# Two convolutions of the next feed-forward step placed between VectorE's additions of the down product

## The chip, the cores and the metric

The kernel runs on one core of a Trainium2 chip. The metric is the device time of one execution in microseconds (us); three executions of the kernel before took 1811.97, 1813.63 and 1813.83 us. A core has TensorE (PE, matmuls into eight PSUM banks), VectorE (DVE), ScalarE (ACT), GpSimd (POOL) and SyncE (SP, which here only issues DMAs). Each engine works through its own list in order; between engines there are semaphores.

## The reference

One inference step of one layer over 1088 tokens (1024 of a new stream, 64 of a running one). After attention and a Conformer convolution comes the feed-forward part, which the change touches:

```python
x = x + (jax.nn.sigmoid(g_attn) * a + jax.nn.sigmoid(g_conv) * c) @ w_out
up, new_ffn = causal_dwconv(rmsnorm(x, norm2_g) @ w_up, ffn_buf, ffn_dw_w, ffn_dw_b)
gate, val = jnp.split(up, 2, axis=-1)
x = x + (jax.nn.silu(gate) * val) @ w_down
```

`w_up` is 1024 x 5632, `w_down` 2816 x 1024; the depthwise convolution has width 3, so its result at a token is a weighted sum of that token and the two before, plus a bias. A final RMSNorm gives the outputs.

## The kernel before

Channels lie on the 128 partitions and tokens along the free dimension. All matmul operands are split into a high and a low part, and each product is three matmuls: high x high and the two mixed ones.

The feed-forward part runs NF = 11 steps. Step i takes two gate tiles and two value tiles of 128 channels each, counted by tau: tau 0 and 2 are gate tiles, tau 1 and 3 value tiles. The tokens are cut into three pieces c of 364, 364 and 360. One *up job* (i, tau, c) is 24 matmuls (`up_product`, L1519) into bank (3 tau + c) mod 4. So there are 12 up jobs per step, and each waits until the bank it writes, used four jobs earlier, has been copied out. The *down product* of the step follows: 18 *down jobs* d, one for each of nine token tiles and two halves of the output columns, six matmuls of 512 columns each (`down_job`, L1294), into banks 4 to 7 in turn. Down job d waits for `down_ev`, that is for VectorE's addition d - 4 out of the same bank:

```python
            if d >= len(banks):
                pe.wait_ge(down_ev, 18 * i + d + 1 - len(banks))
```

An addition (`down_add`, L1304) reads the bank and the residual `x1` and writes the residual.

The order of a step's up jobs is shifted: `steps` gives (i, 1..3, c), then the first gate tile of the next step, (i + 1, 0, c). TensorE, ScalarE and VectorE all go through that list, and TensorE and VectorE then do the down product of step i.

- ScalarE (`window`, and `copy_up` at L1753) copies each up job's bank into `up`; ahead of each copy it does what the job before needs: a sigmoid of a convolved gate piece (`gate_sig`, L1770) or the high part of a finished product (`g_hi`, L1778).
- VectorE (`conv`) makes three passes per piece: L1856 (weight 2 and bias), L1859 and L1862 (the other two weights, each adding to the result so far). Gate pieces go to `cvg`, value pieces to `cvv`. `silu` (L1869) multiplies a gate piece with its sigmoid, `product` (L1876) a value piece with that.
- GpSimd makes the low parts: of products (L1715) and of weights (L1050). ScalarE makes the weights' high parts (L1046) beforehand.

The steps are written out once for i = 0 and i = 10 and as a loop for 1 to 9. There is no scheduler: each engine's order is that of its own function. In step 10 there is no next step, and its final normalisation goes between its additions.

Of the kernel before, what the change touches and what calls it, by code (L numbers as in the profile page):

```python
# [76 lines left out]
def build(nc, a, o, scr):  # L77

    ctx = ExitStack()
    with ctx:  # L80
# [3 lines left out]
        def sem(name):  # L84
            return ctx.enter_context(nc.semaphore(name))
# [31 lines left out]
        def later(n, least=1):  # L117

            return not isinstance(n, int) or n >= least
# [1178 lines left out]
        def down_add(dve, d, i, down_ready, down_ev, banks=(4, 5, 6, 7)):  # L1298
            t, half = d // 2, d % 2
            dve.wait_ge(down_ready, 18 * i + d + 1)  # L1300
            if later(i):
                dve.wait_ge(down_ev, 18 * i + d - 17)
            y = x1[:, t, 512 * half:512 * half + 512]
            dve.tensor_tensor(y, bank[banks[d % len(banks)]][:, :], y, ALU.add).then_inc(down_ev, 1)  # L1304
# [198 lines left out]
        with ExitStack() as c5:  # L1503
# [129 lines left out]
            with ExitStack() as c5b:  # L1633
# [12 lines left out]
                dn_ready, dn_ev = sem("dn_ready"), sem("dn_ev")  # L1646
# [17 lines left out]
                def tile_at(tau, i):  # L1664

                    return FT * (tau % 2) + 2 * i + tau // 2

                def steps(i, last):

                    for tau in (1, 2, 3):  # L1670
                        for c in range(3):
                            yield i, tau, c
                    if not last:
                        for c in range(3):
                            yield i + 1, 0, c

                block = c5b.enter_context(nc.Block())

# [63 lines left out]
                def _(act):  # L1742
# [54 lines left out]
                    def window(i, slots, last=False):  # L1797
                        before = (i, 0, 2)
                        for step in steps(i, last):
                            gating(*before)  # L1800
                            copy_up(*step)
                            before = step
                            k = PREP_AT.get(step[1:], 9)
                            if k < len(slots):
                                prep(i, k, slots[k])
                        if last:
                            gating(*before)
# [26 lines left out]
                @block.vector  # L1834
                def _(dve):
                    def conv(i, tau, c):
                        n0, n1 = NCH[c]
                        n, at, r = n1 - n0, 12 * i + 3 * tau + c, 6 * i + 3 * (tau // 2) + c
                        tile = tile_at(tau, i)
                        dve.wait_ge(up_ev, at + 1)  # L1840
                        if c == 2:
                            dve.wait_ge(up_state, 4 * i + tau + 1)
                        if tau % 2 == 0:
                            dst = cvg[:, c, 0:n]
                            if later(i) or tau >= 2:
                                dve.wait_ge(g_done, r - 2)
                        else:
                            dst = cvv[:, (3 * (tau // 2) + c) % 2, 0:n]
                            if later(r - 1):
                                dve.wait_ge(g_lo_done, r - 1)  # L1850

                        def w(k):
                            return ffw[:, k, ds(tile, 1)]

                        src = up[:, tau % 2, :]
                        dve.tensor_scalar(dst, src[:, n0 + 2:n1 + 2], w(2), prm[:, ds(PRM_FDB + tile, 1)],  # L1856
                                          ALU.mult, ALU.add).then_inc(c2_done, 1)
                        dve.wait_ge(c2_done, at + 1)
                        dve.scalar_tensor_tensor(out=dst, in0=src[:, n0 + 1:n1 + 1], scalar=w(1), in1=dst, op0=ALU.mult,  # L1859
                                                 op1=ALU.add).then_inc(c1_done, 1)  # L1860
                        dve.wait_ge(c1_done, at + 1)
                        dve.scalar_tensor_tensor(out=dst, in0=src[:, n0:n1], scalar=w(0), in1=dst, op0=ALU.mult,  # L1862
                                                 op1=ALU.add).then_inc(cv_done, 1)

                    def silu(i, j, c):
                        n, r = NCH[c][1] - NCH[c][0], 6 * i + 3 * j + c
                        dve.wait_ge(gsig_done, r + 1)
                        dve.wait_ge(cv_done, 12 * i + 6 * j + c + 1)
                        dve.tensor_tensor(cvg[:, c, 0:n], cvg[:, c, 0:n], gsig[:, (3 * j + c) % 2, 0:n],  # L1869
                                          ALU.mult).then_inc(silu_done, 1)  # L1870

                    def product(i, j, c):
                        n, r, x = NCH[c][1] - NCH[c][0], 6 * i + 3 * j + c, (3 * j + c) % 2
                        dve.wait_ge(silu_done, r + 1)
                        dve.wait_ge(cv_done, 12 * i + 6 * j + 3 + c + 1)
                        dve.tensor_tensor(cvv[:, x, 0:n], cvv[:, x, 0:n], cvg[:, c, 0:n], ALU.mult).then_inc(g_done, 1)  # L1876

                    def window(i, last=False):
                        before = (i, 0, 2)
                        for step in steps(i, last):  # L1880
                            if before[1] % 2 == 0:
                                silu(before[0], before[1] // 2, before[2])
                            conv(*step)
                            if step[1] % 2:
                                product(step[0], step[1] // 2, step[2])
                            before = step

                    def final_norm(t):
                        dve.wait_ge(fsd_done, t + 1)
                        dve.reciprocal(rs5[:, NT + t:NT + t + 1], sd5[:, NT + t:NT + t + 1]).then_inc(frs_done, 1)  # L1890
                        dve.wait_ge(frs_done, t + 1)
                        dve.wait_ge(dn_ev, 18 * (NF - 1) + 2 * t + 2)
                        if t >= 2:
                            dve.wait_ge(y_out[t % 2], 16 * (t // 2))
                        dve.scalar_tensor_tensor(out=yst[:, t % 2, :], in0=x1[:, t, :], scalar=rs5[:, NT + t:NT + t + 1],
                                                 in1=gain[:, :], op0=ALU.mult, op1=ALU.mult).then_inc(y_ready, 1)

                    for c in range(3):
                        if c:
                            silu(0, 0, c - 1)  # L1900
                        conv(0, 0, c)
                    window(0)
                    for d in range(18):
                        down_add(dve, d, 0, dn_ready, dn_ev)
                    with dve.Fori(1, NF - 1) as i:
                        window(i)
                        for d in range(18):
                            down_add(dve, d, i, dn_ready, dn_ev)
                    window(NF - 1, True)
                    dve.wait_ge(cv_done, 12 * NF)  # L1910
                    dve.wait_ge(up_tail, 8 * NF)
                    dve.wait_ge(fgain_in, 16)
                    for d in range(18):
                        down_add(dve, d, NF - 1, dn_ready, dn_ev)
                        if d % 2 and d >= 3:
                            final_norm(d // 2 - 1)
                    final_norm(NT - 1)

                @block.tensor
                def _(pe):  # L1920
# [16 lines left out]
                    def window(i, last=False):  # L1937
                        for step in steps(i, last):
                            up_job(*step)
                        slots = LAST5 if last else PREP5  # L1940
                        for d in range(18):
                            down_job(pe, d, (ghi, glo), w_of[4:6], i, dn_ev, dn_ready, g_lo_done, lambda c: 6 * i + 4 + c,
                                     raw5[2], 6 * i + slots.index(5) + 1)
                            if last and d == 3:
                                tails()
# [36 lines left out]
```

## Time and profile before

| | before |
|---|---|
| median of three executions | 1813.63 us |
| lowest, highest | 1811.97, 1813.83 us |
| span of the profiled execution, first to last instruction | 1809.6 us |
| time of the profiled execution outside its span | not shown; the span is 4.0 us under the median |
| mean granted TensorE clock | 0.983 |
| feed-forward steps 1 to 9 | 76.0 or 77.5 us each |

Times inside the trace are counted from the start of the span. A matmul's row gives its start and a modelled duration that reaches into the next matmul, so the pace of a row of matmuls is read from their starts. "Idle before" in brackets is the time in which the engine did nothing ahead of an instruction, with what ended it. The granted clock is a share of TensorE's full speed.

### The profile page before, as it was taken

To read this page: it belongs to the slowest core of one execution; us is meant where nothing else is said; L and a number is where in the kernel's file an instruction comes from. 1 tells how busy PE (TensorE), PEld (TensorE's weight loads), DVE (VectorE), ACT (ScalarE), POOL (GpSimd) and SP (SyncE) were. 2 spreads that over 40 slices of the span, in tenths; PEclk is the share of its full clock that TensorE was granted. 3 is DMA by queue.
4 is the path that set the end of the run, shared out by engine and by line. 5 is a ranking of instruction groups with operands and counts; after the bars stand their busy time and mean duration, and the time that the engine had idled before them with its cause. 6 is when DMAs were issued, how large, how long until landed. Compare 5 with 4: busy or idle time off the path is not lost. (4 is left out here: it accounts for less than half of the span.)

```text
span 1809.6 us, 27060 instructions
## 1 busy us (share of the span) xinstructions
PE 1705.2 (94%) x9642; PEld 1578.0 (87%) x9642; DVE 1195.6 (66%) x1473; ACT 608.2 (34%) x1549; POOL 421.5 (23%) x253
## 2 busy tenths in 40 slices
PE   7899899789889999999999999999999999999998
PEld 6888788678778999989989898988989889898987
DVE  5478888768898425345458765767667676666767
ACT  6335445335444324411134221312213131221314
POOL 3210111010111112333323231413314143131410
PEclk9999999989999999999999999999999999999999
DMA  6320230320231522442222110111101011110202
GB/s 187 90 58 1 73 87 7 99 56 1 83 85 49 171 99 72 182 148 88 87 72 71 47 47 24 58 35 46 46 23 58 23 58 36 33 58 12 69 1 101
DMA packets 145884, 119.47 MB, mean 66 GB/s; under 512 B 6763, under 2 KB 130127, under 8 KB 145800
## 3 DMA queue, kind: packets, MB, share of 16 engines
q1 hardware_dynamic: 145800, 118.35, 21.4%
q8 instruction: 53, 0.87, 0.2%
q14 instruction: 31, 0.25, 0.0%
HBM read 95.83 MB, written 22.50 MB: 65 GB/s over the span
## 5 line engine op out<-in xcount | busy, mean ns | idle before, releaser
L1519 PE MATMUL bank<-h2hi,whi 128*128 128x364 f32 (+1 forms) x1056 | 347.7, 329 | 2.1 <-PEq L1525 2.1
L1519 PE MATMUL bank<-h2hi,wlo 128*128 128x364 f32 (+1 forms) x1056 | 347.7, 329 | 0.0
L1519 PE MATMUL bank<-h2lo,whi 128*128 128x364 f32 (+1 forms) x1056 | 347.6, 329 | 0.0
L1050 POOL TENSOR_TENSOR wlo<-wraw,whi 128x1024 fp32r<-128x1024 f32 x77 | 199.1, 2590 | 623.2 <-ACT whi L1046 622.3
L1304 DVE TENSOR_TENSOR x<-bank,x 128x512 f32<-128x512 f32 x270 | 182.5, 689 | 135.2 <-PE bank L1294 130.8
L1519 PEld LDWEIGHTS bank<-h2hi,whi 128*128 128x128 f32 x1056 | 199.1, 189 | 2.7 <-issue 2.3
L1519 PEld LDWEIGHTS bank<-h2lo,whi 128*128 128x128 f32 x1056 | 199.0, 188 | 0.4
L1519 PEld LDWEIGHTS bank<-h2hi,wlo 128*128 128x128 f32 x1056 | 199.0, 188 | 0.0
L164 POOL TENSOR_TENSOR wlo<-wraw,whi 128x1024 fp32r<-128x1024 f32 x30 | 79.9, 2665 | 493.2 <-ACT whi L174 493.2
L742 DVE SCALAR_TENSOR_TENSOR c_sb<-u,dww,c_sb 128x1118 f32<-128x1118 f32 x120 | 178.2, 1485 | 2.4 <-DVE c_sb L742 1.3
L1294 PE MATMUL bank<-whi,mhi 128*128 128x512 f32 x342 | 136.3, 398 | 33.8 <-DVE x L1304 32.6
L1753 ACT ACTIVATE up<-bank 128x364 f32<-128x364 f32 (+2 forms) x176 | 63.1, 384 | 246.9 <-PE bank L1519 245.4
L1294 PE MATMUL bank<-whi,mlo 128*128 128x512 f32 x342 | 134.7, 394 | 0.0
L1294 PE MATMUL bank<-wlo,mhi 128*128 128x512 f32 x342 | 134.6, 394 | 0.0
L596 ACT ACTIVATE sn<-bank 128x512 f32<-128x512 f32 (+3 forms) x116 | 57.8, 499 | 190.3 <-PE bank L928 151.5
L208 PE MATMUL bank<-whi,hhi 128*128 128x384 f32 x288 | 104.4, 363 | 9.0 <-DVE stage L193 6.0
L1294 PEld LDWEIGHTS bank<-whi,mhi 128*128 128x128 f32 x342 | 65.3, 191 | 52.0 <-DVE x L1304 33.2
L1778 ACT ACTIVATE mhi<-cvv 128x364 fp32r<-128x364 f32 (+1 forms) x88 | 35.5, 427 | 218.9 <-DVE cvv L1876 218.9
L1862 DVE SCALAR_TENSOR_TENSOR cvv<-up,ffw,cvv 128x364 f32<-128x364 f32 (+1 forms) x66 | 101.2, 1534 | 4.5 <-DVE cvv L1859 2.6
L1046 ACT ACTIVATE whi<-wraw 128x1024 fp32r<-128x1024 f32 x77 | 80.4, 1051 | 60.6 <-PE bank L1294 59.3
L208 PE MATMUL bank<-whi,hlo 128*128 128x384 f32 x288 | 99.0, 344 | 0.0
L208 PE MATMUL bank<-wlo,hhi 128*128 128x384 f32 x288 | 98.9, 343 | 0.0
(191 smaller groups left out, 3770.1 us busy)
## 6 DMA issues: line engine op xcount, KB each, us to landing
wraw<-in_w_up SPq DMA_DIRECT2D x88, 256.0 KB, 3.2
wraw<-in_w_in SPq DMA_DIRECT2D x30, 512.0 KB, 5.3
wraw<-in_w_down SPq DMA_DIRECT2D x44, 256.0 KB, 2.7
scr_gate<-gst SPq DMA_DIRECT2D x11, 544.0 KB, 4.2
gch<-scr_gate SPq DMA_DIRECT2D x16, 364.0 KB, 3.9
xt<-in_x_prompt SPq DMA_DIRECT2D x8, 512.0 KB, 5.3
kpast<-in_cache_sb_k SPq DMA_DIRECT2D x16, 256.0 KB, 6.7
vpast<-in_cache_sb_v SPq DMA_DIRECT2D x16, 256.0 KB, 4.8
```

What stands on the lines that cost most here:

```text
L164: pool.tensor_tensor(wlo[:, s, :], wraw[:, s % 2, :], whi[:, s, :].bitcast(F32), ALU.subtract).then_inc(lo_done, 1)
L208: mm = pe.matmul(PJ[t % 2][:, 0:3 * P], x[:, k, tok], w[:, 0:3, ws], start=(k == 0 and n == 0), stop=(k == KT - 1 and n == 2))
L596: act.activation(sn[:, s % 2, 512 - n:512], z, ACT.Sigmoid, scale=-DH ** -0.5)
L742: dve.scalar_tensor_tensor(out=c_sb[:, :], in0=x, scalar=w, in1=c_sb[:, :], op0=ALU.mult, op1=ALU.add).then_inc(tap_done, 1)
L1046: act.activation(dst, wraw[:, parity, :], ACT.Copy).then_inc(sems[1], 1)
L1050: pool.tensor_tensor(dst, wraw[:, parity, :], hi.bitcast(F32), ALU.subtract).then_inc(sems[2], 1)
L1294: mm = pe.matmul(bank[banks[d % len(banks)]][:, :], x[:, k, TOK[t]:TOK[t] + P], w[:, 512 * half:512 * half + 512], start=(k == 0 and n == ...
L1304: dve.tensor_tensor(y, bank[banks[d % len(banks)]][:, :], y, ALU.add).then_inc(down_ev, 1)
L1519: mm = pe.matmul(bank[(3 * tau + c) % 4][:, 0:c1_ - c0], w[:, ws], x[:, k, c0:c1_], start=(k == 0 and n == 0), stop=(k == KT - 1 and n == 2))
L1753: ins = act.activation(up[:, x, x0 + sh + 2:x1_ + sh + 2], bank[(3 * tau + c) % 4][:, x0 - c0:x1_ - c0], ACT.Copy)
L1778: ins = act.activation(ghi[:, j, x0:x1_], cvv[:, (3 * j + c) % 2, x0 + n0:x1_ + n0], ACT.Copy)
L1862: dve.scalar_tensor_tensor(out=dst, in0=src[:, n0:n1], scalar=w(0), in1=dst, op0=ALU.mult, op1=ALU.add).then_inc(cv_done, 1)
```

## The change

`steps` returns a list in place of yielding the same entries. VectorE's `window` takes only the first ten of them: the nine of its own step and piece 0 of the next step's first gate tile. A new function `adds` does the 18 additions, and behind additions 5 and 11 one silu multiplication and one convolution each: `silu` of piece 0 and `conv` of piece 1, then `silu` of piece 1 and `conv` of piece 2. The silu of piece 2 opens the next window, as before. The lists of TensorE, ScalarE, GpSimd and the DMAs are the same. Step 10 is unchanged.

```diff
                 def steps(i, last):
 
-                    for tau in (1, 2, 3):
-                        for c in range(3):
-                            yield i, tau, c
-                    if not last:
-                        for c in range(3):
-                            yield i + 1, 0, c
+                    own = [(i, tau, c) for tau in (1, 2, 3) for c in range(3)]
+                    return own if last else own + [(i + 1, 0, c) for c in range(3)]
...
                     def window(i, last=False):
                         before = (i, 0, 2)
-                        for step in steps(i, last):
+                        for step in steps(i, last)[:10]:
...
+                    def adds(i):
+                        for d in range(18):
+                            down_add(dve, d, i, dn_ready, dn_ev)
+                            if d in (5, 11):
+                                c = d // 6
+                                silu(i + 1, 0, c)
+                                conv(i + 1, 0, c + 1)
...
                     window(0)
-                    for d in range(18):
-                        down_add(dve, d, 0, dn_ready, dn_ev)
+                    adds(0)
                     with dve.Fori(1, NF - 1) as i:
                         window(i)
-                        for d in range(18):
-                            down_add(dve, d, i, dn_ready, dn_ev)
+                        adds(i)
```

VectorE before, from the convolution of the next step's gate piece 0 to the additions. `x` in an addition's row is the residual `x1`; the semaphores are `up_ev` (a piece copied out), `gsig_done` (its sigmoid) and `dn_ready` (a down job done).

```order
L1856 TENSOR_SCALAR cvg<-up,ffw,prm 128x364 [waits g_done,up_ev]
L1859 SCALAR_TENSOR_TENSOR cvg<-up,ffw,cvg 128x364 [waits c2_done]
L1862 SCALAR_TENSOR_TENSOR cvg<-up,ffw,cvg 128x364 [waits c1_done]
L1869 TENSOR_TENSOR cvg<-cvg,gsig 128x364 [waits cv_done,gsig_done]
L1856 TENSOR_SCALAR cvg<-up,ffw,prm 128x364 [waits g_done,up_ev]
L1859 SCALAR_TENSOR_TENSOR cvg<-up,ffw,cvg 128x364 [waits c2_done]
L1862 SCALAR_TENSOR_TENSOR cvg<-up,ffw,cvg 128x364 [waits c1_done]
L1869 TENSOR_TENSOR cvg<-cvg,gsig 128x364 [waits cv_done,gsig_done]
L1856 TENSOR_SCALAR cvg<-up,ffw,prm 128x362 [waits g_done,up_state,up_ev]
L1859 SCALAR_TENSOR_TENSOR cvg<-up,ffw,cvg 128x362 [waits c2_done]
L1862 SCALAR_TENSOR_TENSOR cvg<-up,ffw,cvg 128x362 [waits c1_done]
L1304 TENSOR_TENSOR x<-bank,x 128x512 [waits dn_ready] x18
```

Three convolutions and two multiplications stand ahead of all 18 additions. VectorE after, the same place (lines past `window` are numbered differently; L1852, L1855, L1858 and L1865 are the convolution's passes and the silu multiplication), up to the second group:

```order
L1852 TENSOR_SCALAR cvg<-up,ffw,prm 128x364 [waits g_done,up_ev]
L1855 SCALAR_TENSOR_TENSOR cvg<-up,ffw,cvg 128x364 [waits c2_done]
L1858 SCALAR_TENSOR_TENSOR cvg<-up,ffw,cvg 128x364 [waits c1_done]
L1304 TENSOR_TENSOR x<-bank,x 128x512 [waits dn_ready] x6
L1865 TENSOR_TENSOR cvg<-cvg,gsig 128x364 [waits cv_done,gsig_done]
L1852 TENSOR_SCALAR cvg<-up,ffw,prm 128x364 [waits g_done,up_ev]
L1855 SCALAR_TENSOR_TENSOR cvg<-up,ffw,cvg 128x364 [waits c2_done]
L1858 SCALAR_TENSOR_TENSOR cvg<-up,ffw,cvg 128x364 [waits c1_done]
L1304 TENSOR_TENSOR x<-bank,x 128x512 [waits dn_ready] x6
L1865 TENSOR_TENSOR cvg<-cvg,gsig 128x364 [waits cv_done,gsig_done]
```

Only piece 0 stands ahead of the additions; two groups of a multiplication and three passes have moved behind the sixth and the twelfth addition, and six additions follow the second group.

## Rows read from the trace of the kernel before

**Rows 1.** The page: busy time, share of the span, instructions.
```profile
PE 1705.2 (94%) x9642; PEld 1578.0 (87%) x9642; DVE 1195.6 (66%) x1473; ACT 608.2 (34%) x1549; POOL 421.5 (23%) x253
```

**Rows 2.** PE's waits: us in total, times, longest us.
```profile
PE bank L1294 <- DVE x L1304: 32.6, 11, 3.6
```

**Rows 3.** Two steps, stall to stall: us, busy us by engine, PEclk, DMA.
```profile
1183.40:1259.40 76.00, 72.75 (x396) 68.09 (x396) 51.17 (x68) 18.28 (x48) 22.88 (x14) 1.00 0.14 41
1259.40:1336.90 77.50, 74.31 (x396) 69.24 (x396) 51.12 (x67) 18.27 (x48) 22.88 (x14) 0.98 0.13 41
```

**Rows 4.** PE in order of time: start, us, instruction [idle before <- releaser].
```profile
1030.33 0.47 PE L1294 MATMUL bank<-whi,mhi 128*128 128x512 f32 x1 [1.75 <-DVE x L1304]
...
1106.60 0.50 PE L1294 MATMUL bank<-whi,mhi 128*128 128x512 f32 x1 [3.59 <-DVE x L1304]
...
1256.50 0.39 PE L1294 MATMUL bank<-w5hi,mlo 128*128 128x512 f32 x1
1260.10 0.50 PE L1294 MATMUL bank<-whi,mhi 128*128 128x512 f32 x1 [3.21 <-DVE x L1304]
...
1265.91 0.39 PE L1294 MATMUL bank<-whi,mhi 128*128 128x512 f32 x1
...
1280.87 0.33 PE L1519 MATMUL bank<-h2hi,whi 128*128 128x364 f32 x1
...
1328.77 0.39 PE L1294 MATMUL bank<-whi,mhi 128*128 128x512 f32 x1
...
1334.03 0.39 PE L1294 MATMUL bank<-w5hi,mlo 128*128 128x512 f32 x1
1337.65 0.50 PE L1294 MATMUL bank<-whi,mhi 128*128 128x512 f32 x1 [3.23 <-DVE x L1304]
...
1720.62 0.50 PE L1294 MATMUL bank<-whi,mhi 128*128 128x512 f32 x1 [3.22 <-DVE x L1304]
```

**Rows 5.** One stall and what follows it, by stretches (columns of rows 3).
```profile
1256.73:1260.10 3.37, 0.16 (x1) 0.00 (x0) 2.85 (x6) 1.59 (x6) 0.00 (x0) 1.00 0.00 0
1260.10:1264.55 4.45, 4.45 (x13) 3.51 (x13) 2.43 (x4) 0.00 (x0) 0.00 (x0) 0.62 0.00 0
1264.55:1281.00 16.45, 16.45 (x74) 13.64 (x73) 8.30 (x12) 0.00 (x0) 0.00 (x0) 1.00 0.00 0
```

**Rows 6.** The chain that ended last: start, us, what, after four stalls.
```profile
1184.13 19.38 PE bank L1294 x84
...
1260.10 20.93 PE bank L1294 x84
...
1337.65 19.34 PE bank L1294 x84
...
1413.60 20.97 PE bank L1294 x84
```

**Rows 7.** VectorE in order of time (columns of rows 4).
```profile
1267.56 0.69 DVE L1304 TENSOR_TENSOR x<-bank,x 128x512 f32<-128x512 f32 x1 [0.67 <-PE bank L1294]
...
1328.72 2.51 DVE L1862 SCALAR_TENSOR_TENSOR cvg<-up,ffw,cvg 128x364 f32<-128x364 f32 x1
...
1334.66 0.54 DVE L1869 TENSOR_TENSOR cvg<-cvg,gsig 128x364 f32<-128x364 f32 x1 [0.57 <-ACT gsig L1770]
...
1336.40 0.60 DVE L1862 SCALAR_TENSOR_TENSOR cvg<-up,ffw,cvg 128x362 f32<-128x362 f32 x1
1336.91 3.21 DVE L1304 TENSOR_TENSOR x<-bank,x 128x512 f32<-128x512 f32 x5
```

**Rows 8.** ScalarE in order of time, the copies of pieces 1 and 2.
```profile
1331.77 0.46 ACT L1753 ACTIVATE up<-bank 128x364 f32<-128x364 f32 x1
...
1334.54 0.51 ACT L1753 ACTIVATE up<-bank 128x296 f32<-128x296 f32 x2
```

**Rows 9.** GpSimd in order of time (columns of rows 4).
```profile
1286.64 2.78 POOL L1050 TENSOR_TENSOR wlo<-wraw,whi 128x1024 fp32r<-128x1024 f32 x1 [33.35 <-ACT whi L1046]
...
1328.05 2.79 POOL L1050 TENSOR_TENSOR wlo<-wraw,whi 128x1024 fp32r<-128x1024 f32 x1
```

## The prediction

> **What bounds the kernel now.** I read the page first: TensorE is busy for 94% of the span [rows 1], so the time can only fall where TensorE stands still or runs slowly. Next, who keeps TensorE waiting: the longest total is the down product's matmul (L1294) waiting for VectorE's addition into the residual (L1304), 32.6 us in 11 waits [rows 2]. Next, the feed-forward steps as stretches from one stall to the next: they alternate between 77.5 and 76.0 us, and the granted clock alternates with them, 0.98 and 1.00 [rows 3]; four such pairs stand in a row. Last, TensorE in order of time [rows 4].
>
> A step is 47.9 us of up product without a gap (1280.87 to 1328.77) and 18 down jobs of six matmuls. Four down jobs run (1328.77 to 1334.03); job 4 reuses the bank of job 0, waits for addition 0, and starts only at 1337.65. VectorE shows why [rows 7]: when down job 0 is done it still has two convolutions and the silu multiplications ahead of the additions. Its first addition starts at 1336.91, and TensorE goes on 0.74 us later. There are ten such stalls, one in each step but the last; the first is 1.75 us, the second 3.59, the other eight 3.21 to 3.23 [rows 4].
>
> The stall has a second price. After half of the stalls the 84 matmuls to the end of the down product take 20.93 to 20.97 us, after the others 19.3 to 19.4 [rows 6]. In such a step the granted clock was 1.00 up to and in the stall and 0.62 over the next 4.45 us, which is mostly the lower level of 1.2 GHz; then 2.4 GHz again [rows 5].
>
> **What the change does, part by part.** No engine gets more arithmetic. On VectorE the last two of the twelve convolutions of a step (gate tile of the next step, pieces 1 and 2), each with the silu multiplication ahead of it, leave the place ahead of addition 0 and stand behind additions 5 and 11. TensorE's, ScalarE's and GpSimd's orders and all DMAs stay.
>
> *What is removed.* VectorE ends the convolution of piece 0 at 1328.72 + 2.51 = 1331.23 [rows 7]. Addition 0 can then start at about 1331.25 instead of 1336.91. How late may it be? A job's addition becomes ready 1.65 us after the job's first matmul (1265.91 to 1267.56, rows 4 and 7). A job lasts 1.36 us: 66 matmuls in 1280.87 - 1265.91 = 14.96 us are 0.2267 us each. The bank is needed four jobs later, and the matmul follows the start of the addition by 0.74 us. So an addition may start up to 4 x 1.36 - 0.74 = 4.70 us after its job's first matmul, 3.05 us later than it becomes ready. Addition 0 is ready at 1330.42, due at about 1333.5, and would start at 1331.25: late by 0.8, with 2.2 us to spare. Back to back, additions start 0.63 us apart ((3.21 - 0.69) / 4, rows 7), so VectorE has caught up by addition 2. The stall goes altogether. The next thing that could be late is then an addition behind an inserted group.
>
> *What is inserted.* One group (silu multiplication, then three passes) takes from 1334.66 to 1336.91 = 2.25 us when run back to back [rows 7]. Addition 5 starts on time, 1.65 us after its job's first matmul; the next VectorE instruction can start 0.63 us later; with 2.25 us for the group, addition 6 starts 4.53 us after job 5's first matmul, that is 3.17 after job 6's. It is due at 4.70: 1.5 us to spare. From there the lag shrinks by 0.73 us per addition, so it is gone by addition 9, ahead of the second insertion behind 11, where the sum is the same. In other words a group may last 2.25 + 1.53 = 3.78 us before TensorE feels it.
>
> The moved work also waits. The first group needs ScalarE's sigmoid of piece 0 and its copy of piece 1, the latter at 1331.77 [rows 8], some 6 us before VectorE comes to it (additions 0 to 5 end at about 1337.7). What is queued behind the new wait is on ScalarE: its sigmoid of piece 1 waits for the moved convolution, and behind it stands the copy of piece 2 out of its PSUM bank, which moves from 1334.54 [rows 8] to about 1340.6. It is wanted by the second group at about 1345.8 and, as a bank, by the fourth up job of the next phase; both are later, so I cost it at nothing. The sigmoid of piece 2 moves behind addition 11 and is wanted only after addition 17, 8 us later. The next step's up phase then begins with VectorE, ScalarE and GpSimd standing as they do now.
>
> *What lies beside the moved passes.* A third pass of this convolution took 2.51 us at 1328.72 while GpSimd made the low part of a weight from 1328.05 to 1330.84; the same pass took about 0.6 in the uncontended group [rows 7, 9]. Of GpSimd nothing more runs until 1286.64 + 77.5, after an idle time of 33.35 us [rows 9], so both inserted places are as free of it as the old ones: between 2.25 us and, with both two-input passes stretched by 1.9, 6.05 us. I take 2.25, the row of these very instructions beside an idle GpSimd. The Trainium skill, GPSIMD Engine Reference, section Key points, says that GpSimd shares its SBUF interfaces with VectorE and contends with instructions of two SBUF inputs. By that rule, the 2.51 us row agrees, and the pass that stays ahead of the additions keeps its stretch; the result is the same.
>
> **The sum.**
> 1. Standing still: the idle rows count from a matmul's modelled end; from start to start 1260.10 - 1256.50 = 3.60, less the 0.23 that a matmul takes anyway, is 3.37, or 0.16 more than the row's 3.21. Ten stalls: 1.75 + 3.59 + 8 x 3.23 = 31.2, plus 10 x 0.16 = 32.8 us.
> 2. Slow restart: 84 matmuls at 0.2267 are 19.04 us. From first start to the start of the up product they took 1280.87 - 1260.10 = 20.77 [rows 4], 0.16 less than the chain's piece of 20.93. So the five slow ones lose 20.95 - 0.16 - 19.04 = 1.75 each, 8.7 us; the other five lose 19.34 - 0.16 - 19.04 = 0.14 each, 0.7. Together 9.4 us.
> Sum 42.2 us. The same from the steps: one would last 47.9 + 5.48 (four down jobs, from 1328.77 to where a fifth would start) + 19.04 = 72.42 us; now it is (1720.62 - 1106.60) / 8 = 76.75 [rows 4]. Eight times 4.33 is 34.7; outside that stretch lie the first two stalls (1.91 and 3.75) and two restarts (0.14 and 1.75): 42.2 again.
>
> The profiled span is 1809.6 us, 4.0 under the median of the three times shown, 1813.63; what lies around the span I leave as it is. Span after: 1767.4; time: 1771.4 us, say 1771.
>
> **The clock term.** Of the 9.4 us, 8.0 are the five slow recoveries (1.6 each over an undisturbed restart). The rows show that each stands right behind a stall, and that the 48 us of up product and the rest of the down product run at 1.00. The Trainium skill, TensorE: Matmul & The Clock Gate, Part 1, says that activity keeps the throttle released and idleness brings it back. By that rule the dips go with the stalls; the rows agree in that none is seen without one, but only half of the stalls have one, so this is the least certain term.
>
> **Rivals.**
> - *The clock dips stay*, every second step, for a cause that is not the stall. For it: they come strictly in turn. Against: they never begin while TensorE works. 1771 + 8 = 1779 us. Chance 0.05.
> - *An inserted group lasts longer than its 3.78 us*, so TensorE stalls at down jobs 10 and 16 instead of 4. With one pass stretched as in the 2.51 us row a group is 4.15 us: 0.4 x 20 = 7 us, 1778; something between that and 1790 with longer waits. Against: no GpSimd work there. Chance 0.07.
> - *The stall only shrinks*: piece 0's convolution ends later than now because something in the up phase slips. A slip of 2.2 us is free, each further one costs itself; with 2 us left of each stall, 1790 to 1795. Chance 0.03. That the change does not do what it says I can exclude: VectorE's order shows six additions ahead of the moved group.
> - *Slower*: both two-input passes of both groups stretched, or each group held by ScalarE's queue, in which the copy of the next piece stands behind a sigmoid that waits for VectorE. At 6.05 us a group stalls TensorE by 2.27; 20 of them are 45 us, with a slow restart behind some of them 1817 to 1825. It decides from where 20 stalls eat the 42.2 us: 3.78 + 2.11 = 5.9 us per group. Against: the copy has some 5 us in hand. Chance 0.03.
>
> **How the numbers follow.** The forecast, all stalls gone and clock even, has 0.82: 1768 to 1774. The range reaches to the kept dips and to a little stalling in the middle: 1765 to 1784. Around 0.2% of the time, 3.6 us, is what a measurement tells from no change. Only the last rival is slower (0.03); between cases a chance of 0.02 falls within that bound; 0.95 are faster.
>
> **What would show it.** Right: TensorE's waits for L1304 fall from 32.6 to about 1.5 us; steps of 72.4 us, all alike, clock 1.00; addition 0 starts 2.4 us after the first down matmul, addition 6 3.2 us after its job's; ScalarE's sigmoid (L1770) waits some 7 us for VectorE once per step; the groups last 2.3 us. Wrong: a wait of TensorE at down job 10 or 16, or at an up job for a bank not copied out; groups above 3.8 us; a clock below 1.00 in a step without a stall; an up phase over 48 us.

## The result and the profile after

| | before | after |
|---|---|---|
| median (executions) | 1813.73 us (4) | 1767.68 us (4) |
| lowest, highest | 1811.97, 1814.46 | 1766.05, 1771.58 |
| ratio, with its 95% interval | | 0.9734 [0.9706, 0.9762] |
| span of the profiled execution | 1809.6 us | 1769.8 us |
| feed-forward part, first up job after the change of blocks to the end | 840.1 us | 798.0 us |
| ten down products with a next step | 287.3 us | 245.2 us |

The forecast was 1771 us, faster, with a range of 1765 to 1784; the measured 1767.68 lies in it, 0.3 us under the 1768 to 1774 that the prediction gave its main case. Timed again, the changed kernel took 1767.78 us and the kernel before 1817.19, ratio 0.9727 [0.9695, 0.9758].

The page of the changed kernel answers to [rows 1]: TensorE is now busy for 96% of a span 40 us shorter, VectorE does the same work.

```profile
PE 1694.6 (96%) x9642; PEld 1574.0 (89%) x9642; DVE 1192.9 (67%) x1473; ACT 608.3 (34%) x1549; POOL 420.2 (24%) x253
```

TensorE's waits after, longest first (us in total, times, longest). The 32.6 us of [rows 2] no longer lead the list; the waits at its head belong to the attention and the first norm. What is left for an addition at L1304 is 2.1 us in two waits, both ahead of the feed-forward part (the prediction said some 1.5).

```profile
PE bank L928 <- DVE sg L789: 20.9, 9, 5.7
PE bank L402 <- DVE xt L363: 14.0, 2, 11.7
PE bank L917 <- issue: 6.6, 1, 6.6
...
PE bank L1294 <- DVE x L1304: 2.1, 2, 1.1
```

Two steps after, from the first down matmul of one to that of the next (columns of [rows 3]), and one down product and one up phase apart. TensorE is busy without a break, the clock is 1.00 in each, and the steps are alike, where they were 76.0 and 77.5.

```profile
1170.08:1242.50 72.42, 72.42 (x397) 68.17 (x397) 50.78 (x67) 18.29 (x48) 22.88 (x15) 1.00 0.14 43
1242.50:1314.92 72.42, 72.42 (x398) 68.17 (x397) 50.77 (x67) 18.29 (x48) 22.88 (x15) 1.00 0.14 43
1314.92:1339.44 24.52, 24.52 (x109) 20.27 (x109) 17.78 (x26) 2.71 (x9) 2.05 (x1) 1.00 0.07 21
1339.44:1387.34 47.90, 47.90 (x290) 47.90 (x288) 33.00 (x41) 15.57 (x39) 20.82 (x14) 1.00 0.18 55
```

The chain that ended last (start, us, what), where [rows 6] had a piece of VectorE between every two of TensorE's: it is TensorE alone.

```profile
1267.18 47.90 PE bank L1519 x288
1315.08 24.52 PE bank L1294 x108
1339.60 47.90 PE bank L1519 x288
```

VectorE in order of time, over that down product (its first matmul starts at 1314.92). This answers to [rows 7]: addition 0 starts at 1317.28, 2.36 us after the first matmul, instead of 8.14; the first group stands from 1324.02 to 1326.11.

```profile
1314.85 2.51 DVE L1858 SCALAR_TENSOR_TENSOR cvg<-up,ffw,cvg 128x364 f32<-128x364 f32 x1
1317.28 1.38 DVE L1304 TENSOR_TENSOR x<-bank,x 128x512 f32<-128x512 f32 x2
1319.33 0.69 DVE L1304 TENSOR_TENSOR x<-bank,x 128x512 f32<-128x512 f32 x1 [0.67 <-PE bank L1294]
...
1323.41 0.69 DVE L1304 TENSOR_TENSOR x<-bank,x 128x512 f32<-128x512 f32 x1 [0.67 <-PE bank L1294]
1324.02 0.53 DVE L1865 TENSOR_TENSOR cvg<-cvg,gsig 128x364 f32<-128x364 f32 x1
...
1325.60 0.60 DVE L1858 SCALAR_TENSOR_TENSOR cvg<-up,ffw,cvg 128x364 f32<-128x364 f32 x1
1326.11 2.07 DVE L1304 TENSOR_TENSOR x<-bank,x 128x512 f32<-128x512 f32 x3
1328.85 0.69 DVE L1304 TENSOR_TENSOR x<-bank,x 128x512 f32<-128x512 f32 x1 [0.67 <-PE bank L1294]
```

The reader is to see the idle times in brackets: two additions after the start VectorE waits for TensorE again, and after the group, from the fourth addition on.

ScalarE in the same stretch, answering to [rows 8]. Its sigmoid of piece 1 now waits 7.78 us for the moved convolution, and the copy of piece 2 is behind it, at 1326.64. The sigmoid of piece 2 waits 6.90 us in the same way. TensorE waits for neither.

```profile
1317.89 0.46 ACT L1749 ACTIVATE up<-bank 128x364 f32<-128x364 f32 x1
...
1326.23 0.51 ACT L1766 ACTIVATE gsig<-cvg 128x364 f32<-128x364 f32 x1 [7.78 <-DVE cvg L1858]
1326.64 0.51 ACT L1749 ACTIVATE up<-bank 128x296 f32<-128x296 f32 x2
...
1334.47 0.51 ACT L1766 ACTIVATE gsig<-cvg 128x362 f32<-128x362 f32 x1 [6.90 <-DVE cvg L1858]
```

### The profile page after: what moved, and what is told of

Read it like the earlier page. It is cut to its first block and busy times, and to the rows that moved or that the text cites. A ratio compares the mean times of both kernels' runs of the same rounds, so it can differ in the third digit from the quotient of the medians.

```text
span 1769.8 us, 27060 instructions
## 1 busy us (share of the span) xinstructions
PE 1694.6 (96%) x9642; PEld 1574.0 (89%) x9642; DVE 1192.9 (67%) x1473; ACT 608.3 (34%) x1549; POOL 420.2 (24%) x253
## 5 line engine op out<-in xcount | busy, mean ns | idle before, releaser
L1304 DVE TENSOR_TENSOR x<-bank,x 128x512 f32<-128x512 f32 x270 | 183.1, 688 | 109.3 <-PE bank L1294 103.4
L1766 ACT ACTIVATE gsig<-cvg 128x364 f32<-128x364 f32 (+1 forms) x66 | 33.6, 508 | 257.2 <-DVE cvg L1858 257.2
L1858 DVE SCALAR_TENSOR_TENSOR cvv<-up,ffw,cvv 128x364 f32<-128x364 f32 (+1 forms) x66 | 101.2, 1534 | 4.5 <-DVE cvv L1855 2.6
L1711 POOL TENSOR_TENSOR mlo<-cvv,mhi 128x364 fp32r<-128x364 f32 (+1 forms) x88 | 75.3, 871 | 93.0 <-ACT mhi L1774 93.0
```

What stands on the lines that cost most here:

```text
L1711: ins = pool.tensor_tensor(glo[:, j, x0:x1_], cvv[:, (3 * j + c) % 2, x0 + n0:x1_ + n0], ghi[:, j, x0:x1_].bitcast(F32), ALU.subtract)
```

## The experiments

The length of a step's down product is read from the starts of its first matmul and of the next up product's first. It costs 24.52 us when nothing is in its way. The sum over the ten down products that have a next step, less 245.2, is called the loss; before it is 42.1 us, after it is 0. It is a better measure here than the time, since the part ahead of the feed-forward part moved by some 3.6 us from trace to trace whatever the kernel (first up job at 968.2 to 971.8).

| kernel | time, us | ratio to before, 95% | down product of a middle step, us | loss, us |
|---|---|---|---|---|
| before | 1809 to 1824 | 1 | 28.05 or 29.65 | 42.1 |
| after, again | 1767.78 | 0.9727 [0.9695, 0.9758] | 24.52 | 0.0 |
| one group moved | 1774.43 | 0.9790 [0.9764, 0.9816] | 25.13 | 5.9 |
| both groups behind addition 5 | 1781.68 | 0.9806 [0.9774, 0.9837] | 25.85 | 13.1 |
| groups 2.0 us longer | 1777.95 | 0.9787 [0.9756, 0.9819] | 25.43 | 9.1 |
| groups 1.0 us longer | 1769.28 | 0.9759 [0.9725, 0.9793] | 24.52 | 0.0 |
| 3 passes ahead of addition 0 | 1768.89 | 0.9757 [0.9722, 0.9791] | 24.52 | 0.0 |
| 8 passes | 1787.14 | 0.9852 [0.9824, 0.9881] | 26.37 | 17.6 |
| 11 passes | 1821.33 | 1.0025 [1.0003, 1.0047] | 30.62 | 55.1 |
| 15 passes | 1844.82 | 1.0143 [1.0115, 1.0171] | 31.2 to 32.8 | 73.6 |
| before, stall filled | 1802.56 | 0.9916 [0.9891, 0.9942] | 28.04 | 34.9 |
| before, stall half filled | 1810.30 | 0.9963 [0.9947, 0.9979] | 28.04 or 29.68 | 42.2 |
| GpSimd beside a group | 1770.38 | 0.9726 [0.9697, 0.9755] | 24.54 | 0.3 |

Each ratio is to executions of the kernel before from the same round of runs. Their medians differ: 1817.19 us (for "after, again", "both groups", "2.0 us longer" and "stall filled"), 1811.89 (for "one group", "1.0 us longer", 3 and 8 passes) and 1815.26 (for the others). The times of "1.0 us longer" and of 3 passes are of two executions each, so what is said of these two rests on their traces.

**The changed kernel again.**

> The changed kernel once more, unchanged. Theory (ten stalls and the slow restarts behind them are gone, 42.2 us of the feed-forward part): the feed-forward part from its first up job in this trace is again about 42 us shorter than before, and what the whole time differs by more or less than that lies ahead of it, where the two kernels are the same. Rival (the change gains more than 42 us, since the median fell by 46): the feed-forward part is 46 us shorter.

Measured: the feed-forward part is 798.0 us, 42.1 less than before, as in the first trace. The rival falls for these traces: what the medians differ by beyond 42 is not in them (see the clock, below).

**One group alone.**

```diff
-                        for step in steps(i, last)[:10]:
+                        for step in steps(i, last)[:11]:
...
-                            if d in (5, 11):
-                                c = d // 6
+                            if d == 11:
+                                c = 1
```

> Half of the change: only the convolution of piece 2 (with the silu multiplication of piece 1) moves, behind addition 11; that of piece 1 stays ahead of addition 0. Theory (an addition 0 that starts at 1333.5 on the clock of the trace before costs nothing, each us beyond it costs one): it would start at 1334.0 to 1334.1, so a stall of 0.5 to 0.6 us is left in the steps 1 to 9, none in step 0, and with the restarts the time is some 6 us over the changed kernel, 1774. Rival (gain in proportion to the work moved): half of 42 us, 1789.

Measured: 1774.43 us, loss 5.9; no stall in step 0, 0.71 us of idle time in step 1, 0.32 in the others. TensorE in this kernel:

```profile
1318.36 0.50 PE L1294 MATMUL bank<-whi,mhi 128*128 128x512 f32 x1 [0.32 <-DVE x L1304]
```

```profile
1317.62 1.28 DVE L1304 TENSOR_TENSOR x<-bank,x 128x512 f32<-128x512 f32 x2
```

VectorE starts addition 0 at 1317.62, 0.74 us ahead of that matmul, as before. With 0.16 for the modelled end the stall is 0.48 us. The restart costs 0.13 more (the first matmul of it is followed after 0.34 us instead of 0.23), and together they are the 0.61 by which 25.13 exceeds 24.52. The gain is not in proportion to the work moved: the first of two equal groups brings 36 us, the second 6.

**Both groups in one place.**

```diff
-                            if d in (5, 11):
-                                c = d // 6
-                                silu(i + 1, 0, c)
-                                conv(i + 1, 0, c + 1)
+                            if d == 5:
+                                for c in range(2):
+                                    silu(i + 1, 0, c)
+                                    conv(i + 1, 0, c + 1)
```

> The changed kernel with both groups behind addition 5, none behind 11. Theory (a group may last 3.78 us before TensorE waits, and the second of two groups in a row waits about 0.57 us for ScalarE's sigmoid): the double group lasts 5.0 us, TensorE stands still 1.2 us at down job 10 of ten steps, 13 us more than the changed kernel with the restarts, about 1781. Rival A (ScalarE's wait is hidden, group 4.5 us): 0.7 us a step, 8 us, 1776. Rival B (more slack than reckoned): no stall, 1768.

Measured: 1781.68 us, loss 13.1. VectorE between addition 5 and addition 6, with ScalarE's sigmoid in the middle:

```profile
1178.52 0.53 DVE L1865 TENSOR_TENSOR cvg<-cvg,gsig 128x364 f32<-128x364 f32 x1
...
1181.27 0.54 DVE L1865 TENSOR_TENSOR cvg<-cvg,gsig 128x364 f32<-128x364 f32 x1 [0.58 <-ACT gsig L1766]
...
1183.51 3.21 DVE L1304 TENSOR_TENSOR x<-bank,x 128x512 f32<-128x512 f32 x5
```

The two groups together last 4.99 us, 1.21 over the limit of 3.78; with the restart that makes 1.34, and the down product is 1.33 longer. Both rivals fall. So the two groups need two places: without the 0.58 us that VectorE waits for the second sigmoid they would still last some 4.4 us (an estimate, 4.99 less 0.58).

**Longer groups.** The first pass is repeated, each repetition behind the one before it; n is 4 in one kernel and 2 in the other, both in `conv` as called from `adds` (`extra` and `done` are new arguments of `conv`).

```diff
+                        for m in range(extra):
+                            dve.tensor_scalar(dst, src[:, n0 + 2:n1 + 2], w(2), prm[:, ds(PRM_FDB + tile, 1)],
+                                              ALU.mult, ALU.add).then_inc(ex_done, 1)
+                            dve.wait_ge(ex_done, done + m + 1)
...
-                                conv(i + 1, 0, c + 1)
+                                conv(i + 1, 0, c + 1, n, 2 * n * i + n * c)
```

> The changed kernel with the first pass of both moved convolutions done five times instead of once: each group is four passes of 0.51 us longer, 4.3 us instead of 2.25. Theory (limit 3.78 us per group): TensorE waits 0.5 us at down jobs 10 and 16 of ten steps, 10 us or, with a short restart each, 13 us more than the changed kernel, about 1780. Rival (the slack is larger, and the prediction's margin of 1.5 us was cautious): 1768. Second rival (the time goes with VectorE's work): 20 x 2.04 = 41 us more, 1809.

> The changed kernel with the first pass of both moved convolutions done three times: each group lasts 3.3 us instead of 2.25, under the limit of 3.78. Theory: no wait of TensorE in the down product, feed-forward part as long as in the changed kernel. Rival (every us of VectorE in the down product counts): 20 us more.

Measured with four: the group lasts 4.12 us, and each costs TensorE 0.46 us, that is 0.34 over the limit and 0.13 for the restart; 20 of them 9.1 us. VectorE around the second group:

```profile
1114.10 0.53 DVE L1869 TENSOR_TENSOR cvg<-cvg,gsig 128x364 f32<-128x364 f32 x1
1114.55 1.98 DVE L1853 TENSOR_SCALAR cvg<-up,ffw,prm 128x362 f32<-128x362 f32 x4
...
1118.22 3.21 DVE L1304 TENSOR_TENSOR x<-bank,x 128x512 f32<-128x512 f32 x5
```

With two the group lasts 3.10 us and there is no loss at all, though VectorE has 20 us more to do.

**A later addition 0.** The same repetitions in the convolution that stays ahead of the additions: 3, 8, 11 and 15.

```diff
-                            conv(*step)
+                            if step[1]:
+                                conv(*step)
+                            else:
+                                conv(*step, n, n * i)
```

> The changed kernel with the first pass of the convolution that stays ahead of addition 0 done four times: addition 0 starts 1.5 us later. Theory (2.2 us to spare): no stall. Rival (less slack): up to 15 us more.

> The same with nine times: addition 0 starts 4.1 us later, 1.8 us past its limit. Theory: TensorE stands still 1.8 us at down job 4 of ten steps, 18 us and 1 to 2 for the restarts over the changed kernel, 1788. For the clock: in the kernel before, a stall of 1.9 us had no dip behind it and of nine stalls of 3.4 to 3.8 us five had one. If it is the length of the stall that matters, there is no dip here; if only the turn of the steps, there are five, and 8 us more, 1796.

> The changed kernel with the first pass of the convolution ahead of addition 0 done twelve times: addition 0 starts 5.6 us later than in the changed kernel, as late as in the kernel before; the moved groups stay moved. Theory (the whole gain is the stall at down job 4 and what the clock does behind it): the stall is 3.3 us again, dips follow some of the stalls again, and the time is the kernel before's, 1810 to 1820. Rival (part of the gain comes from the moved groups themselves): 1800 or less.

> The same with sixteen times: 2 us more stall, 5.3 us in each of ten steps. Theory of the clock (the longer TensorE stands still, the surer the clock falls behind it): a dip behind nearly every stall, where stalls of 3.3 us had one behind about half and stalls of 1.7 us none; down product 24.5 + 5.4 + 1.7 = 31.7 us in nearly every step, time 1768 + 10 x 7 = 1838. Rival (dips come by turns whatever the length): 1830, with 30.0 and 31.7 alternating.

With three passes addition 0 starts 3.93 us after the first down matmul, in place of 2.36, which is the 1.5 us later that was meant; in step 1 it is 4.31. Both are short of the 4.70 us that the prediction has as the limit, and no step has a stall.

```profile
1313.50 0.39 PE L1294 MATMUL bank<-whi,mhi 128*128 128x512 f32 x1
```

```profile
1312.61 2.94 DVE L1853 TENSOR_SCALAR cvg<-up,ffw,prm 128x364 f32<-128x364 f32 x2
...
1316.91 0.60 DVE L1862 SCALAR_TENSOR_TENSOR cvg<-up,ffw,cvg 128x364 f32<-128x364 f32 x1
1317.43 2.54 DVE L1304 TENSOR_TENSOR x<-bank,x 128x512 f32<-128x512 f32 x4
```

The repetitions took the place beside GpSimd, so that one of them was stretched and the third pass of the convolution itself, 2.51 us in the changed kernel, took 0.60. So 1.6 of the 2.2 us to spare were used here without a loss, and eight passes go over them: addition 0 starts 6.46 us after the first down matmul, 1.76 past the limit. The idle times were 1.55 to 1.93 us in nine steps and 0.19 in the first, no dip of the clock, loss 17.6; 18 and 1 to 2 for the restarts were expected. The time is 19.5 us over the changed kernel's.

With eleven, addition 0 starts 8.00 us after the first down matmul (8.14 before) with both groups still moved. The stall at down job 4 is back, 3.1 us of idle time for 3.2, and so is the time: 1821 us, a little over the kernel before (1815.26 beside it).

```profile
1576.62 2.48 DVE L1304 TENSOR_TENSOR x<-bank,x 128x512 f32<-128x512 f32 x4
```

```profile
1577.36 0.80 PE L1294 MATMUL bank<-whi,mhi 128*128 128x512 f32 x1 [3.10 <-DVE x L1304]
```

Standing still makes up 31.4 us of this kernel's loss of 55.1, against 32.8 of 42.1 before. The rival falls; nothing of the gain comes from the new places as such. The rest of the loss is the slow clock behind nine of the ten stalls (see the last section). With fifteen each of the ten stalls had a dip, as expected, but of unequal size; the time, 1844.82 us, is above both forecasts (1838 and 1830), since a dip cost up to 2.9 us there and not 1.7.

**The kernel before with the stall filled.** `again` is 2 (filled) or 1 (half filled) for down job 3 of the steps 0 to 9.

```diff
-            for k in range(2):
+            for k in [0, 1] * (1 + again):
```

> The kernel before, with down job 3 of the steps 0 to 9 computed three times in its bank instead of once (its sum starts anew each time, so the result is that of the last): 12 more matmuls, 2.7 us of work, in the place where TensorE stood still for 3.4 us. Theory (the clock falls because of the stall): the dips to 0.62 are gone, each of the steps 2 to 9 lasts 76 us or less, and the time is 8 us under before in spite of the added work (1806, ratio 0.9956); step 0, whose stall was only 1.9 us, gets 0.8 longer. Rival (the dips have another cause and come every second step anyway): dips stay and the time is that of before, 1814, or 1 us more.

> The kernel before with down job 3 of the steps 0 to 9 computed twice (its sum starts anew, so the result is that of the last): 6 more matmuls, 1.4 us, and a stall of 2.0 us left. Theory: TensorE goes on when addition 0 allows, so the down product keeps its length of 28.05 us in the steps without a dip; a remaining stall of 2.0 us is like the 1.9 us one of step 0 and the 1.7 us ones behind a late addition 0, which had no dip: 1802 to 1804, as with the stall nearly filled. Rival (the dips need a stall of 3.4 us in sum of parts, or come anyway): 1810 and more.

Filled: TensorE does 12 matmuls more per step and the kernel gets faster, 1802.56 us. Steps 2 to 9 have an idle time of 0.50 us, their down products all last 28.03 to 28.07 us, the length of an undisturbed one before, and the clock is 1.00 throughout:

```profile
1182.74:1258.72 75.98, 75.47 (x409) 70.35 (x409) 51.14 (x67) 18.31 (x48) 22.86 (x14) 1.00 0.14 41
1258.72:1334.65 75.93, 75.43 (x408) 70.34 (x408) 51.14 (x67) 18.30 (x48) 22.87 (x14) 1.00 0.14 41
```

Trace against trace the loss falls by 7.3 us: 8.0 for five dips, less 0.7 in step 0. The medians differ by 14.6 us (1817.19 for the kernel before in that round), twice as much as the traces; this is the same open difference as between 42 and 49 us above. The rival, a clock that falls by turns whatever TensorE does, falls.

Half filled: the expectation failed. It was 1802 to 1804 us; the median of ten executions is 1810.30, which is the rival's number and 5 us under before. The idle times were 1.87 us (2.25 in step 1, 0.39 in step 0), and the clock fell behind five of the ten stalls all the same; the loss in the trace is the 42.2 us of before. One such stall:

```profile
1565.99 0.50 PE L1295 MATMUL bank<-whi,mhi 128*128 128x512 f32 x1 [1.87 <-DVE x L1305]
...
1567.18 0.63 PE L1295 MATMUL bank<-w5lo,mhi 128*128 128x512 f32 x1
1567.61 0.63 PE L1295 MATMUL bank<-w5hi,mlo 128*128 128x512 f32 x1
```

The matmuls start 0.43 us apart there, where 0.23 is usual. A stall need not be 3 us long to cost a dip.

**GpSimd beside a group.**

```diff
+                        if len(slots) > 5:
+                            pool.wait_ge(dn_ready, 18 * i + 6)
                         prep(5)
```

> The changed kernel with GpSimd's last job of a step (the low part of a weight, 2.8 us) held back until down job 5 is done, so that it runs beside the first moved group. Theory (VectorE's passes with two inputs are stretched to the end of GpSimd's instruction, as the pass of 2.51 us was): the first group lasts some 4.1 us instead of 2.1, over the limit of 3.78; TensorE waits 0.3 to 0.5 us at down job 10, 4 to 6 us more in all; and the last pass of piece 0's convolution, which stood beside GpSimd before, lasts 0.6 us and addition 0 starts 1.9 us earlier. Rival (the 2.51 us had another cause): group 2.1 us, no stall, 1768.

VectorE in that kernel: the first instruction of the group is stretched from 0.53 to 2.13 us while GpSimd works from 1178.73 to 1181.12, and the pass ahead of the additions, at 1170.23, takes 0.60.

```profile
1170.23 0.60 DVE L1860 SCALAR_TENSOR_TENSOR cvg<-up,ffw,cvg 128x364 f32<-128x364 f32 x1
...
1178.77 0.69 DVE L1304 TENSOR_TENSOR x<-bank,x 128x512 f32<-128x512 f32 x1 [0.67 <-PE bank L1294]
1179.38 2.13 DVE L1867 TENSOR_TENSOR cvg<-cvg,gsig 128x364 f32<-128x364 f32 x1
...
1183.07 2.48 DVE L1304 TENSOR_TENSOR x<-bank,x 128x512 f32<-128x512 f32 x4
```

```profile
1178.73 2.39 POOL L1050 TENSOR_TENSOR wlo<-wraw,whi 128x1024 fp32r<-128x1024 f32 x1 [9.20 <-PE bank L1294]
```

The stretch is confirmed, its size was over-rated: 3.69 us a group instead of 4.1. That is 0.09 under the limit, and TensorE hardly waits: the down product is 0.03 us longer in most steps and 0.13 in step 0. Addition 0 starts 1.68 us after the first down matmul, only 0.7 earlier than in the changed kernel and not 1.9 as expected, since it now waits for down job 0 itself. The rule of the Trainium skill (GPSIMD Engine Reference, Key points) is that GpSimd and VectorE contend where VectorE's instruction has two SBUF inputs. These rows agree: the multiplication that now stands beside GpSimd takes 2.13 us in place of 0.53, and the pass that no longer does takes 0.60 in place of 2.51.

## Why the prediction was right, step by step

- *Where the time was*: right. The stall at down job 4 of ten steps is gone, and with eleven passes put in its way and the groups left where they are it comes back with its full price.
- *Addition 0 on time*: forecast 2.4 us after the first down matmul, measured 2.36 (2.72 in step 1). The limit of 4.70 us lies between the starts that cost nothing (3.93 and 4.31 us, three passes) and those that cost a stall (5.22 with one group, 6.46 with eight passes); in the latter TensorE goes on 0.74 us after addition 0, as reckoned.
- *The group*: forecast 2.25 us, measured 2.09; the first pass starts 0.44 us after the silu multiplication, in place of 0.60 in the row that the forecast took. So addition 6 starts 2.99 us after its job's first matmul instead of 3.2. Limit 3.78 us: bracketed from below by 3.10 (no loss) and 3.69 (0.03 us), and met from above by 4.12 and 4.99, whose losses give 3.78 again.
- *ScalarE's queue*: it costs nothing, as reckoned. The prediction had one wait of some 7 us per step; there are two, 7.78 and 6.90.
- *The sum*: 42.2 us forecast, 42.1 in the trace (287.3 - 245.2). The forecast was worked out from this same trace of the kernel before, so this shows that all of its loss was removed, and nothing of how other executions fare. Its parts, stall 32.8 and restarts 9.4, hold as a sum; the filled stall bears out the 8 us of the clock in it.
- *The time*: 1771.4 forecast, 1767.68 measured. The term that was mis-sized is the 4.0 us "around the span". Where an execution's span and time are both listed they lie 1.7 to 1.9 us apart (1771.58 and 1769.8), so the profiled execution of before took about 1811.4 us, at the low end of its kernel. By 1.8 the forecast would be 1769.2. The other 1.5 us are within what the part ahead of the first up job moves between executions (3.6 us).
- *The clock*: "the dips go with the stalls" held. One argument for it was misread: the prediction says that the dips never begin while TensorE works. In the trace of before each of the five begins 0.7 to 1.1 us after TensorE has gone on, as [rows 5] allow (1.00 in the stall, 0.62 after it). They do begin only behind a stall, and that is what decides. What the forecast took from one trace, five dips of 1.6 us, is not fixed. Of the kernel before 37 more executions are listed with clock and span; the span goes with the clock, from 1807.5 us at 0.984 to 1822.4 at 0.975. The changed kernel's eight times lie within 1765.3 and 1771.6, its clocks within 0.987 and 0.990. So the spread is 15 us before and 6 after, though over fewer executions. I take it that this is why the medians differ by 46 or 49 us and the profiled executions' feed-forward parts by 42. That is not shown: there are no traces of the slower executions.

## What to carry to other kernels

When an engine finishes its side work late and then clears a backlog, compare the deadline of the first item (buffers times the pace of the producer, less the hand-over) with its start, and move only what lies past it into the gaps that the consumer has while it keeps pace. Size each moved piece by the same rule: here up to 3.78 us between two additions cost nothing, and each us beyond costs one, twenty times. A wait of TensorE cost more than its length here: 0.13 us for each restart, and 1.3 to 2.9 us where the clock fell. So a stall is worth removing even where the engine only stands for 2 us.

## What was not expected of the hardware

**The price of a stall in clock is not a function of its length.** Idle times of TensorE in the traces, and the dips behind them:

| idle time, us | kernel | dips | cost of one, us |
|---|---|---|---|
| 0.5 and 0.9 | before, stall filled | none of 9 | |
| 0.9 to 1.0 | both groups behind addition 5 | none of 10 | |
| 1.55 to 1.93 | 8 passes | none of 9 | |
| 1.75 | before and 11 passes, step 0 of each | none of 2 | |
| 1.86 to 2.25 | before, stall half filled | 5 of 9 | 1.6 |
| 3.2 to 3.6 | before | 5 of 9 | 1.6 |
| 3.1 to 3.5 | 11 passes | 9 of 9 | 1.6 in two, 2.7 in seven |
| 3.7 to 5.5 | 15 passes | 10 of 10 | 1.3 to 2.9 |

So a stall of 1.93 us in one kernel had no dip, and stalls of 1.87 us in another had one. One step of the kernel with eleven passes (columns of [rows 3]) shows why a dip can cost more than in [rows 5]:

```profile
1573.90:1577.36 3.46, 0.36 (x3) 0.01 (x1) 3.12 (x7) 0.54 (x2) 0.00 (x0) 0.85 0.00 0
1577.36:1578.90 1.54, 1.54 (x4) 1.25 (x5) 1.54 (x3) 0.42 (x2) 0.00 (x0) 0.50 0.00 0
1578.90:1583.00 4.10, 4.10 (x11) 3.22 (x10) 0.92 (x3) 0.00 (x0) 0.00 (x0) 0.50 0.00 0
1583.00:1590.00 7.00, 7.00 (x32) 5.73 (x31) 5.26 (x9) 1.24 (x5) 0.00 (x0) 0.99 0.00 0
```

Here the clock fell to its lower level, 1.2 GHz, while TensorE still stood, and stayed there for all of the 5.6 us after it went on; matmuls of 512 columns start 0.43 us apart instead of 0.23. In [rows 5] the stall itself was at 1.00, and only the part after it was slow. The stretch of [rows 5] after the stall, cut where the clock fell, 0.8 us after TensorE had gone on:

```profile
1260.10:1260.90 0.80, 0.80 (x3) 0.67 (x4) 0.80 (x2) 0.00 (x0) 0.00 (x0) 1.00 0.00 0
1260.95:1264.30 3.35, 3.35 (x10) 2.59 (x9) 1.58 (x3) 0.00 (x0) 0.00 (x0) 0.50 0.00 0
```

What decides between these stays open: no run here varied a stall's length without its place in the step, or the reverse.

**GpSimd can cost VectorE more than the overlap seems worth, and once only.** An instruction of 0.53 or 0.60 us that starts while GpSimd works on a weight's low part ends 0.4 us after GpSimd's (2.13 and 2.51 us); the ones behind it have their usual length. One that is already running when GpSimd starts keeps its length: the pass ahead of the 2.51 us one, 0.60 us from 1327.98 in the trace of before, where GpSimd starts at 1328.05. So does the addition at 1178.77 above, one of whose inputs is a PSUM bank: 0.69 us beside GpSimd's instruction from 1178.73. Two tensor inputs are not needed for a stretch: in the run with three passes a pass with one (TENSOR_SCALAR) took it (2.94 us for two), and the two-input pass behind was spared.
